# A decoder step on one Trainium2 core: the recurrent stage's input products by one level of Strassen's algorithm, its steps laid out between half pairs, and no reciprocal

## The reference

```python
u_rnn, u_gate, g_a, g_b = columns of x @ w_in        # 1024 wide each
xc = conv_b + sum(up[:, k:k+T] * conv_w[k] for k in range(4))
r  = sigmoid(xc @ w_rg_a + b_rg_a)                   # 8 diagonal blocks of 128
i  = sigmoid(xc @ w_rg_i + b_rg_i)
a  = exp(-8 * r * softplus(-lambda))
b  = sqrt(1 - a*a) * (i * xc)                        # -expm1(2 log a)
h[t] = a[t] * h[t-1] + b[t]
R  = h * gelu(u_gate)
x1 = LN(alpha*x + (sigmoid(g_a)*(A @ Wa) + sigmoid(g_b)*(R @ Wb)) @ w_out)
```

## Time and profile before

| | |
|---|---|
| median of three runs | 2316.95 us (2316.89 to 2318.61) |
| the profiled execution's own time | 2318.44 us |
| its span in the profile | 2316.5 us |
| mean granted TensorE clock | 0.983 |
| PE busy | 2219.7 us, 96% of the span |
| DVE busy | 960.4 us, 41% |
| ACT busy | 633.2 us, 27% |
| share of the chain that ended last | PE 88%, DVE 7%, DMA 2%, ACT 1% |
| chain, by line | L1409 19%, L1224 13%, L1420 10%, L1152 10% |

### The profile page before, as it was taken

The page is one execution under the profiler, slowest core; times in us unless marked ns, Lnnn a source line. Parts: engine busy times, 40 slices in busy tenths (PEclk is TensorE's granted clock), DMA queues, the critical chain, the costliest instruction groups (busy, mean ns, idle before and its releaser), DMA issues.

```text
span 2316.5 us, 28210 instructions
## 1 busy us (share of the span) xinstructions
PE 2219.7 (96%) x9940; PEld 1369.6 (59%) x9940; DVE 960.4 (41%) x1972; ACT 633.2 (27%) x1347; POOL 455.1 (20%) x890
## 2 busy tenths in 40 slices
PE   8998999999999998999999999899999999999986
PEld 6455665667666665888886556444444545454542
DVE  0226888844356667335443558511111111111116
ACT  2125665644434433111111221011111111111112
POOL 0002444300100000000000000033434344443430
PEclk9998999999999999999999999999999999999997
DMA  6302000244511111101312114499999999999945
GB/s 209 111 14 87 2 2 1 76 180 174 193 48 35 37 28 38 37 28 46 109 55 97 73 46 174 178 325 346 343 360 332 352 343 347 347 347 335 346 109 220
DMA packets 133211, 378.21 MB, mean 163 GB/s; under 512 B 23891, under 2 KB 81355, under 8 KB 105835
## 3 DMA queue, kind: packets, MB, share of 16 engines
q1 hardware_dynamic: 109587, 292.46, 34.0%
q0 software_dynamic: 23520, 84.36, 12.7%
HBM read 341.48 MB, written 58.00 MB: 172 GB/s over the span
## 4 chain that ended last, share of the span: by engine, by line
PE 88%; DVE 7%; DMA 2%; ACT 1%; issue 1%; SPq 0%; POOL 0%; DVEq 0%; ACTq 0%; POOLq 0%
PE PS L1409 19%; PE PS L1224 13%; PE PS L1420 10%; PE PS L1152 10%; PE PS L740 8%; PE PS L853 5%; PE PS L1322 4%; PE PS L886 3%; PE PS L923 3%; PE PS L1306 2%; PE PS L1023 2%; PE PS L788 1%; PE PS L1361 1%; PE PS L1208 1%; DVE arena L2048 1%
## 5 line engine op out<-in xcount | busy, mean ns | idle before, releaser
L1409 PE MATMUL PS<-arena 128*128 128x512 f32 x1040 | 457.2, 592 | 0.8 <-ACT arena L1498 0.8
L1498 ACT ACTIVATE arena<-PS 128x512 f32<-128x512 f32 (+11 forms) x583 | 266.4, 472 | 694.8 <-PE PS L740 422.6
L740 PEld LDWEIGHTS PS<-arena 128*128 128x128 f32 (+3 forms) x1950 | 234.6, 159 | 193.7 <-issue 129.7
L1224 PE MATMUL PS<-arena 128*128 128x258 f32 x1456 | 319.6, 383 | 10.8 <-ACT arena L1766 7.6
L1409 PEld LDWEIGHTS PS<-arena 128*128 128x128 f32 x1040 | 192.9, 190 | 218.8 <-issue 217.8
L740 PE MATMUL PS<-arena 128*128 128x128 f32 (+3 forms) x1950 | 287.5, 278 | 36.1 <-DVE arena L2024 8.1
L1224 PEld LDWEIGHTS PS<-arena 128*128 128x128 f32 x1456 | 277.8, 191 | 52.7 <-issue 8.0
L1152 PE MATMUL PS<-arena 128*128 128x344 f32 x864 | 251.8, 453 | 0.0
L1420 PE MATMUL PS<-arena 128*128 128x512 f32 x520 | 239.2, 593 | 0.5 <-ACT arena L1498 0.5
L1152 PEld LDWEIGHTS PS<-arena 128*128 128x128 f32 x864 | 163.9, 190 | 86.0 <-ACT arena L1750 0.4
L2454 DVE TENSOR_TENSOR arena<-PS,arena 128x256 f32<-128x256 f32 x65 | 27.6, 425 | 432.4 <-ACT arena L1832 425.7
(11 more groups left out here) (337 smaller groups left out, 2247.1 us busy)
## 6 DMA issues: line engine op xcount, KB each, us to landing
arena<-in_w_exp_gate SPq DMA_DIRECT2D x65, 1024.0 KB, 7.6
arena<-in_w_exp_up SPq DMA_DIRECT2D x65, 1024.0 KB, 10.9
arena<-in_w_exp_down SPq DMA_DIRECT2D x65, 1024.0 KB, 9.4
arena<-in_w_in SPq DMA_DIRECT2D x34, 512.0 KB, 4.0
arena<-in_x_prompt SPq DMA_DIRECT2D x16, 512.0 KB, 3.6
expert_rows<-arena SPq DMA_DIRECT2D x16, 512.0 KB
arena<-expert_rows SPq DMA_DIRECT2D x6, 1024.0 KB, 12.2
arena<-in_w_in SPq DMA_DIRECT2D x16, 256.0 KB, 7.4
```

The lines of the kernel that those rows point to most:

```text
L740: return nc.tensor.transpose(out, in_, ident[0:n, 0:n])
L1224: ins = mm(PS[:, bank, 0:QT], lhs[:, l0 + k, :], right[:, r0 + k, c0:c0 + QT], start=first and k == 0, stop=k == kh - 1, skip_group_check= ...
L1409: ins = mm(PS[:, 2 + s, :].rearrange("p (h n) -> p h n", h=2), xgT[:, s, k, :], up_w[w][:, :, k, :], start=k == 0, stop=k == KT - 1)
L1498: return fn(out, in_, ACT.Copy)
```

## The change

- The first blocks of u and gate stay direct products. The other seven u blocks and seven gate blocks become seven Strassen pairs, of a new kind "ux". The first block of g_a and g_b joins its kind (now "gx"), so that there are 23 pairs: 7 ux, 4 wb, 4 wa, 8 gx. Their order is u1 u2 | g1 g2 | u3 u4 | g3 g4 | u5 u6 | g7 u7 | g5 g6.
- The gates r and i of block n are issued behind unit `AFTER`: 0, 2, 3, 6, 7, 10, 11 and 12 for n = 0 to 7. They use 4 matmuls of 258 columns into the other unit's banks (r) and into those of the unit just finished (i). The convolutions run in units 2, 6, 10 (two each) and 12 (one).
- The sums of x's right operand are made once, in front of the first pair, and are used again at the end by "gx", of which only the second part is made anew. In a unit the order of the second and third product is exchanged, and waits on single sums replace a wait on all four.
- The reciprocal and the two operations around it become one Square on ScalarE and one operation on VectorE (`norm_input`). The scan writes straight into R, and gelu is applied in place, by halves, after the adds of a gate unit.
- The eight small transposes go into one place behind pair 7; the meeting of the engines ahead of the pairs goes away. SP loads the weights of r and i later, between the second and the third ring slot.

The diff, cut to its core (`targets`, the order of the ring, the sizes of the tiles, SP's conditions, the removed lines of ScalarE and some others are left out):

```diff
--- before.py
+++ after.py
...
+        PAIRS = [(2 + 2 * i, ("ux" if i < 7 else "wb" if i < 11 else "wa" if i < 15 else "gx")) for i in range(23)]
+        YB, YA, GX = 7, 11, 15
+        AFTER = {0: 0, 2: 1, 3: 2, 6: 3, 7: 4, 10: 5, 11: 6, 12: 7}
+        CONV = {2: (1, 2), 6: (3, 4), 10: (5, 6), 12: (7,)}
+        GELU = {2: slice(1, 3), 3: slice(1, 3), 6: slice(0, 2), 7: slice(0, 2), 10: slice(1, 2), 11: slice(1, 2), 12: slice(0, 3, 2), 13: slice(0, 3, 2)}
+        GG_AT = {0: 0, 1: 1, 2: 2, 3: 0, 4: 1, 7: 1, 5: 2, 6: 0}
+        G_EV = {0: 1, 1: 3, 2: 3, 3: 5, 4: 5, 7: 7, 5: 9, 6: 9}
+        GATED = {1: (0,), 4: (1, 2), 8: (3, 4)}
...
-        T_AT = {"wb": 0, "wa": 2, "in": 4}
+        T_AT = {"ux": 0, "wb": 8, "wa": 16, "gx": 22}
...
+                    if u - 1 in AFTER:
+                        pe.wait_ge(sem("r_ev"), AFTER[u - 1] + 1)
+                    elif u - 2 in AFTER:
+                        pe.wait_ge(sem("i_ev"), AFTER[u - 2] + 1)
+                    if u >= 2:
                         pe.wait_ge(st_ev, PEV * (u - 1))
-                        pe.wait_ge(st_cb, ADD * (u - 2) + 1)
...
+                        pe.wait_ge(st_cb, ADD * (u - 1))
...
+                    if i == YB:
+                        pe.wait_ge(sem("stg_done"), 4)
+                    E.do(prod(bank, w1, 0, rhs, 0, c0, True), st_mm)
+                    pe.wait_ge(sem("t_done"), t + 1 + j)
+                    pe.wait_ge(sem("s_done"), i + 1)
+                    if i == YB + 1 and j == 0:
+                        pe.wait_ge(sem("stg_ev"), 2)
+                    E.do(prod(bank + 2, s1, 0, rhs, 0, c1, True), st_mm)
+                    if i == YB:
                         pe.wait_ge(sem("stg_done"), KT)
...
                     E.do(prod(bank + 1, w1, kh, rhs, kh, c0, True), st_mm)
...
                     pe.wait_ge(st_ev, PEV * u + 1)
+                    pe.wait_ge(sem("t_done"), t + 3 + 3 * j)
                     E.do(prod(bank, s2, 0, t2, 0, c0, False), st_mm)
+                    pe.wait_ge(sem("t_done"), t + 4 + 3 * j)
+                    if u == 0:
+                        pe.wait_ge(sem("g_ev"), 1)
                     E.do(prod(bank + 3, w2, 0, t3, 0, c0, True), st_mm)
                     pe.wait_ge(st_ev, PEV * u + 2)
                     E.do(prod(bank + 2, s4, 0, rhs, kh, c1, False), st_mm)
+                    pe.wait_ge(sem("t_done"), t + 5 + 3 * j)
                     pe.wait_ge(st_cb, ADD * u + 2)
-                    ins = prod(bank + 3, w2, kh, t4, 0, c0, False)
-                    E.do(ins, st_mm)
...
+                    E.do(prod(bank + 3, w2, kh, t4, 0, c0, False), st_mm)
+                    if u in AFTER:
+                        gates_of(AFTER[u], u, bank)
+
+            def gates_of(n, u, bank):
+
+                other_bank = 4 - bank
+                pe.wait_ge(sem("xc_done"), n + 1)
+                if n == 0:
+                    pe.wait_ge(sem("g_ev"), 1)
+                    pe.wait_ge(sem("win_read"), 3)
+                    pe.wait_ge(sem("win_in"), (BD + 9) * 16)
+                else:
+                    pe.wait_ge(sem("i_ev"), n)
+                    pe.wait_ge(sem("r_ev"), n)
+                    pe.wait_ge(st_ev, PEV * u)
+                    pe.wait_ge(st_cb, ADD * u)
+                for c in range(4):
+                    ins = mm(PS[:, other_bank + c, 0:QT], wra[:, n, :], xc[:, n % 2, c * QT:(c + 1) * QT], start=True, stop=True)
+                E.do(ins, sem("r_mm"))
+                pe.wait_ge(st_ev, PEV * (u + 1))
+                pe.wait_ge(st_cb, ADD * (u + 1))
+                for c in range(4):
+                    ins = mm(PS[:, bank + c, 0:QT], wri[:, n, :], xc[:, n % 2, c * QT:(c + 1) * QT], start=True, stop=True)
+                E.do(ins, sem("i_mm"))
...
+            act.wait_ge(w_used, 2)
+            E.do(fn(gg[:, 0, :].rearrange("p (a b) -> p a b", a=3), PS[:, 3:6, 0:CH], ACT.Gelu_apprx_tanh), sem("g_ev"))
+
+            def gelu_of(u):
+
+                act.wait_ge(st_cb, ADD * (u + 1))
+                g = gg[:, GELU[u], :].rearrange("p h (t j c) -> p h t j c", t=2, j=2)[:, :, :, u % 2, :]
+                E.do(fn(g, g, ACT.Gelu_apprx_tanh), sem("g_ev"))
+
+            for i in range(len(PAIRS)):
                 d1, d2 = targets(i)
                 for j in range(2):
                     u, bank = 2 * i + j, 4 * j
+                    n = AFTER.get(u - 1)
+                    if n is not None:
+                        act.wait_ge(sem("r_mm"), n + 1)
+                        if n:
+                            act.wait_ge(sem("hs_done"), n)
+                        E.do(fn(rr.rearrange("p (a b) -> p a b", a=4), PS[:, bank:bank + 4, 0:QT], ACT.Sigmoid, bias=vec[:, n, 37:38]), sem("r_ev"))
+                        act.wait_ge(sem("i_mm"), n + 1)
+                        E.do(fn(ii.rearrange("p (a b) -> p a b", a=4), PS[:, 4 - bank:8 - bank, 0:QT], ACT.Sigmoid, bias=vec[:, n, 38:39]), sem("i_ev"))
                     act.wait_ge(st_mm, PROD * u + 1)
-                    if i >= 8:
-                        act.wait_ge(sem("mg_done"), max(1, u - 16))
+                    if j == 0 and i in (0, 2, 4):
+                        act.wait_ge(sem("xc_done"), i + 1)
+                    if j == 0 and i in (3, 5, 6):
+                        act.wait_ge(sem("stg_done"), 2 if i == 3 else 5)
+                    if i >= GX and u - 2 * GX >= 2:
+                        act.wait_ge(sem("mg_done"), u - 2 * GX - 1)
                     E.do(copy(quarter(d1, 0, j), PS[:, bank, 0:QT]), st_ev)
-                    act.wait_ge(st_mm, PROD * u + 3)
+                    if n is not None:
+                        E.step(fn(aa, rr, ACT.Exp, scale=lam[:, 3, n:n + 1]))
+                        E.do(fn(RT[:, n, :], aa, ACT.Square))
+                        E.do(fn(rr, rr, ACT.Tanh, scale=lam[:, 4, n:n + 1]), sem("a_done"))
+                    act.wait_ge(st_mm, PROD * u + 2)
+                    if i == 5 and j == 0:
+                        act.wait_ge(sem("xc_done"), 6)
                     E.do(copy(quarter(d2, 1, j), PS[:, bank + 2, 0:QT]), st_ev)
                     act.wait_ge(st_mm, PROD * u + 4)
                     E.do(copy(quarter(d1, 1, j), PS[:, bank, 0:QT]), st_ev)
-                    if i >= 8:
+                    if n is not None:
+                        act.wait_ge(sem("v_done"), n + 1)
+                        E.do(fn(rr, rr, ACT.Sqrt), sem("sq_done"))
+                    if u - 1 in GELU and u < 2 * YB:
+                        gelu_of(u - 1)
+                    if u == 2 * YB - 1:
...
+            def gated_input(n):
+                dve.wait_ge(sem("i_ev"), n + 1)
+                E.do(tt(ii, ii, xc[:, n % 2, :], ALU.mult))
+
+            def norm_input(n):
                 dve.wait_ge(sem("a_done"), n + 1)
-                E.step(ts(vv, th, 1.0, None, ALU.add))
-                E.step(V.reciprocal(vv, vv))
-                E.step(stt(vv, th, 2.0, vv, ALU.mult, ALU.mult), sem("v_done"))
-                E.step(tt(ii, ii, xc, ALU.mult))
+                E.step(stt(rr, RT[:, n, :], 1.0, rr, ALU.add, ALU.mult), sem("v_done"))
+
+            def recur(n):
                 dve.wait_ge(sem("sq_done"), n + 1)
-                E.step(tt(ii, ii, vv, ALU.mult))
-                E.do(V.tensor_tensor_scan(hs[:, 0:SEQ], aa[:, 0:SEQ], ii[:, 0:SEQ], 0.0, ALU.mult, ALU.add))
-                E.step(tt(hs[:, SEQ:NTOK], aa[:, SEQ:NTOK], vec[:, n, 24:32], ALU.mult))
-                E.step(tt(hs[:, SEQ:NTOK], hs[:, SEQ:NTOK], ii[:, SEQ:NTOK], ALU.add))
-                E.do(V.tensor_copy(stg[:, 11:20], hs[:, SEQ - 1:NTOK]))
-                E.step(tt(RT[:, n, :], hs, gg[:, n % 2, :], ALU.mult), sem("stg_done"))
-
-            def right_sums(kind, j):
+                E.step(tt(ii, ii, rr, ALU.mult))
+                E.do(V.tensor_tensor_scan(RT[:, n, 0:SEQ], aa[:, 0:SEQ], ii[:, 0:SEQ], 0.0, ALU.mult, ALU.add))
+
+            def recur_rows(n):
+                E.step(tt(RT[:, n, SEQ:NTOK], aa[:, SEQ:NTOK], vec[:, n, 24:32], ALU.mult))
+                E.step(tt(RT[:, n, SEQ:NTOK], RT[:, n, SEQ:NTOK], ii[:, SEQ:NTOK], ALU.add))
...
+            def gate_rows(n):
+                dve.wait_ge(sem("g_ev"), G_EV[n])
+                E.step(tt(RT[:, n, :], RT[:, n, :], gg[:, GG_AT[n], :], ALU.mult), sem("stg_done"))
+
...
+            def right_first(kind):
+
+                x, kh, _ = OPERAND[kind]
+                for j in range(2):
+                    c0, c1 = slice(j * QT, (j + 1) * QT), slice(HT + j * QT, HT + (j + 1) * QT)
+                    E.step(tt(x[:, 0:kh, c1], x[:, 0:kh, c1], x[:, 0:kh, c0], ALU.subtract), sem("t_done"))
+
...
+                for j in range(2):
+                    c0, c1 = slice(j * QT, (j + 1) * QT), slice(HT + j * QT, HT + (j + 1) * QT)
+                    E.step(tt(t2[:, :, c0], x[:, kh:2 * kh, c1], x[:, 0:kh, c1], ALU.subtract), sem("t_done"))
+                    E.step(tt(t3[:, :, c0], t2[:, :, c0], x[:, 0:kh, c0], ALU.subtract), sem("t_done"))
```

(90 more changed lines are left out.)

207 lines of the change are left out of this document (72 added, 135 removed).

## The result

| | before | changed |
|---|---|---|
| median, first comparison (6 runs each) | 2317.36 us | 2303.24 us |
| ratio, 95% interval | | 0.9939 [0.9924, 0.9953] |
| median, second comparison (9 and 4 runs) | 2317.54 us | 2301.63 us |
| ratio, 95% interval | | 0.9931 [0.9911, 0.9951] |
| the profiled execution: time, span | 2318.44, 2316.5 us | 2302.16, 2300.3 us |

The change makes the kernel 14 to 16 us faster. One of the four runs of the changed kernel in the second comparison took 2522.05 us at a mean granted clock of 0.864; the ratio leaves it out. The forecast was 20.7 us, to 2296.

The account below looks back on a forecast made before the run. PE was taken to set the time. 26.9 + 3.1 + 9.8 + 3.3 - 20.4 - 2.0 = 20.7 us less, from 2316.95 to 2296 us; range 2289 to 2306.

Parts of the forecast that it names:

- PE's work: Multiplying in pairs wins 3.36 us for each of eight pairs, 26.9 us; moving the eight transposes wins 3.1 more.
- Waits that go: PE's waits vanish ahead of the pairs (9.8 us, half-clock start included) and at the last pairs' operand sums (3.3 us).
- Waits that come: New PE waits in the first unit, behind blocks and convolutions, and at R's operand sum to 20.4 us.
- the gelu product's: At the first wb pair, PE waits 3.3 us for a second sum and three gelu products before reading R's lower half.
- The third at the wb unit: At the first wb pair, six other sums and two adds outlast four products, so PE waits 1.5 us.
- The clock: Behind the new long waits, one stretch of 4 us at half clock, 2.0 us lost.
- rival B: More of the new waits in units 2 to 14 end at half clock: 6 to 9 us back, 2302 to 2305; chance 0.17.
- The signs of being wrong: Wrong if: table load before Square; waits over 30 or under 14 us; ux clock below 0.97; L1322 shift outside 15-30 us.
- C: At gate i, a longer ScalarE chain in each block, as from Square's own table: 2308 to 2316 us; chance 0.08.
- D: New waits shorter, as VectorE overlaps more: a third of 20.4 us gone and no clock loss give 2288; chance 0.08.
- E: Slower: TensorE does not regain full clock between waits; 45 us at half clock in the ux pairs eat the gain; chance 0.03.
- F: Time within 0.2%: the longer block chain at its upper end plus more half clock, 2313 to 2321 us; chance 0.04.

Follow-up runs that it names:

- the version with the exact form alone: The kernel before, with only the reciprocal replaced by Square on ScalarE and one VectorE operation; 2310.58 us, ratio 0.9971 to the kernel before.

## Why the prediction was right or wrong

**PE's work: right.** From the chain of waits behind the first wb pair:

```profile
909.96 1.03 PE PS L761 x8
910.99 316.70 PE PS L1226 x1456
```

316.70 us for 1456 instructions are 0.2175 each, 24.36 for a pair; 3.4 us are won for each of eight pairs, 27.2 against 26.9. The eight transposes take 1.03 us in one place where 2.5 were put: 1.5 better.

**Waits that go: right.** The 7.6 us with the half-clock start, and the 2.8 us at the operand of the last pairs, are gone (new waits at the first wb pair stand in the next paragraph); the changed kernel's PE has no wait at all in these 316.70 us.

**Waits that come: the mechanism right, one term too small.** Of the 13 waits laid out, 12 are found where they were put. The one behind the second convolution of unit 2 was put at 3.4 and is 3.1. In the timeline of the changed kernel:

```profile
703.50 0.17 DVE L2251 COPY arena<-arena 128x11 f32<-128x11 f32 x1
703.71 0.43 DVE L2328 TENSOR_TENSOR arena<-PS,arena 128x258 f32<-128x258 f32 x1
...
704.39 0.42 DVE L2331 TENSOR_TENSOR arena<-PS,arena 128x258 f32<-128x258 f32 x1
704.96 1.98 PE L1290 MATMUL PS<-arena 128*128 128x258 f32 x8 [3.13 <-DVE arena L2331]
```

The convolution ends, three adds follow, and gate i starts. Behind units 3, 7 and 11 it is 0.6, as laid out. The step that failed is the sentence "So PE waits 0.6 behind units 3, 7 and 11, and not where no gate follows". It counted VectorE's adds and left out ScalarE's sigmoid of r, on which the next unit's first product waits, for its banks. I had taken the table load to run ahead of every wait, as it does in the kernel before; there one of the sigmoid's two waits was always met long before. In the changed kernel it is the sample tokens' rows, which come 0.5 us behind the adds. Four waits (3.5 + 1.0 us) come of it; the run with that wait moved took them away. The first sum's wait (2.4 laid out, 2.35 found) and the gelu product's (3.3 and 3.1) fit; the one behind unit 12 was put at 1.8 and is 1.1. The third at the wb unit (1.5) did not appear. The 1.7 us lost at half clock behind the gelu product's wait (3.4 us at 0.50) cover it; the two versions in which these products ran at full clock show it with 1.49 us.

**The clock: too small.** One stretch with 2.0 us lost was put in; 6.8 us at half clock in the first profile (3.4 lost) and 10.2 in the second (5.1 lost) were found. The prediction took the length of a wait for the sign, with 2.8 us as harmless. The runs do not bear this out: waits of 2.2 us were followed by half clock too. In the first profile of the changed kernel, one of the two stretches at 0.50 (826.5 to 829.9) stands behind gate i's wait of 2.24 behind unit 10, while the same wait behind unit 6 and the one of 3.1 behind unit 2 were followed by full clock. Four microseconds behind the operand's wait, in the first profile (columns as above):

```profile
888.00:892.00 4.00, 4.00 (x13) 3.19 (x12) 3.86 (x5) 0.00 (x0) 0.00 (x0) 0.59 0.00 0
```

This is a part of rival B, with 1.4 to 3.1 us beyond the 2.0 put in where B had 6 to 9.

**The sum again.** 591.1 less 20.7 is 570.4; the middle part measured 574.9, which is 4.5 more, and 576.6 in the second profile, 6.2 more. Toward it the first profile gives:

- 1.4 us of listed waits: 4.5 for the sigmoid, less 1.5 for the third wait at the wb unit, 0.7 for unit 12 and 0.9 for the small differences of the others;
- 2.6 us because each of the 16 waits costs 0.16 more than the list says;
- 1.4 for the clock (3.4 instead of 2.0), in the second profile 3.1;
- 1.5 less for the transposes and 0.3 less for the pairs.

This makes 3.6, and 5.3 for the second profile; 0.9 us of each stay open. That the time fell into the range is in part luck: the four sigmoid waits that were left out, and the clock, were partly made good by a wait that did not appear and by the transposes. The case that was named for 2301 to 2305, B, is right in its cause only for a smaller part of the miss.

**The signs of being wrong.** None came in that bears on the change: no table load stands before Square, the listed waits sum to 21.8, the clock in the ux stretch is 0.99, and L1351 starts 20.0 us earlier than L1322 did. The rest of the kernel was to stay within 2 us. Its two parts moved by 3.8 each in the first profiles, and by 1.2 and 0.7 in the second, so this is the spread between profiles.

**The rivals.** C named gate i as the place where a late ScalarE goes to PE, with Square's table as the cause. Square has no table of its own, so C as it was put did not happen. The reciprocal put back shows the price of that chain, but in another place: 41.6 us at the middle add, and 6.7 at gate i. The Trainium skill ("ScalarE: Activation LUTs", What ACT_TABLE_LOAD costs) has about 1380 ns of drain for a change of table besides the load. The loads shown here have none on either side: the load at 721.96 ends at 723.24 and the sigmoid starts at 723.26, and the load at 718.31 of the run with the changed wait starts 0.02 us behind the gelu in front of it (717.23 + 1.06). D did not happen. E did not happen to this version. The one with the reciprocal has 44.4 us at half clock, about the 45 that E names, and is slower than before; but its waits alone, 34.2 us more than in the changed kernel, would make it so. F did not happen.

## What to carry to other kernels

An operation that costs little beside the bound engine can cost most of its length once the order is tightened: the same reciprocals are worth 6.7 us in the old order and 47 in the new one, some 34 of them as waits and the rest as lost clock. Lay out each engine's order in front of a wait: an add for PE belongs ahead of long work for the next step, and moving three convolutions, each behind three adds, was worth more than half of what the whole change brought (8.9 us in the middle part, against 16.1). And look at what a table load waits for: of two waits in front of an activation, one may hold the load.

## What the runs showed of the hardware

- A table load can be held by a wait in front of its activation. With one of two waits open it started 0.08 us behind that wait's end (721.88, 721.96), and the activation came 1.3 us later.
- The length of a single wait of TensorE did not decide what the clock did. In the middle parts, waits of 2.2 to 3.1 us were followed by half clock in some executions and not in others of the same kernel: the wait of 3.1 behind unit 2 in the second profile of the changed kernel and not in the first, the one of 2.24 behind unit 10 in the first and not in the second. A wait of 3.0 ahead of the pairs, in the version with the exact form alone, cost no clock at all. The 7.6 us in the kernel before were followed by 0.50 in both profiles.
- With twenty waits between 640 and 960 us, 56.0 us in all and the longest 6.9, the clock stood at 1.2 GHz for 44.4 us, the longest time at a stretch being 6.8. Each of the eight waits of 4.6 us or more among them was followed by it.
